# Mixing weights fetched as rows from DRAM in place of 48 transposes, with the order of some late work changed

## The reference

```
h = x + 0.5 * swiglu(rms_norm(x))                      # width 2816
z = rms_norm(h) @ w_in + b_in                          # aq ak av bq bk bv ga gb
ya = dilated attention, 12 heads in 3 groups           # windows 128/512/2048, dilations 1/4/16
yb = sliding-window attention, 8 query heads, sinks
merged = sigmoid(ga) * (ya @ w_branch_a) + sigmoid(gb) * (yb @ w_branch_b)
h = h + merged @ w_out
h = h + 0.5 * swiglu(rms_norm(h))
out = rms_norm(h)
```

## Time and profile before

| what | us |
|---|---|
| median of 3 runs | 2035.16 (2033.75 to 2035.31) |
| the profiled execution's own time | 2035.47 |
| its span | 2033.7 |
| PE busy | 2011.3 (99%), 9374 matmuls |
| DVE busy | 1361.3 (67%) |
| ACT busy | 784.6 (39%) |
| POOL busy | 83.7 (4%) |

### The profile page before, as it was taken

The page is one execution under the profiler, slowest core; times in us unless marked ns, Lnnn a source line. Parts: engine busy times, 40 slices in busy tenths (PEclk is TensorE's granted clock), DMA queues, the critical chain, the costliest instruction groups (busy, mean ns, idle before and its releaser), DMA issues.

```text
span 2033.7 us, 26354 instructions
## 1 busy us (share of the span) xinstructions
PE 2011.3 (99%) x9374; PEld 1640.7 (81%) x9374; DVE 1361.3 (67%) x2333; ACT 784.6 (39%) x1479; POOL 83.7 (4%) x94
## 2 busy tenths in 40 slices
PE   8999999999999999999999999999999999999998
PEld 6888888888888877777777888888888888888886
DVE  7986666666988455555666443458876676666986
ACT  6343333334455243334454112135433333334453
POOL 1000000000012100100100000000000000000021
PEclk9999999999999999999999999999999999999999
DMA  5233333258544311101114111114233323267433
GB/s 187 78 120 124 120 132 108 92 173 282 158 126 151 105 39 45 34 32 43 48 58 145 55 53 47 48 46 150 99 109 109 104 99 109 78 228 251 142 95 128
DMA packets 97563, 221.23 MB, mean 109 GB/s; under 512 B 20159, under 2 KB 20195, under 8 KB 95648
## 3 DMA queue, kind: packets, MB, share of 16 engines
q1 hardware_dynamic: 69568, 164.66, 24.5%
q10 hardware_dynamic: 22800, 46.29, 6.7%
q0 software_dynamic: 5072, 8.68, 1.3%
HBM read 164.41 MB, written 59.08 MB: 110 GB/s over the span
## 4 chain that ended last, share of the span: by engine, by line
PE 95%; DVE 3%; ACT 1%; issue 1%; DMA 0%; ACTq 0%; DVEq 0%; SPq 0%
PE bank L2017 20%; PE bank L2019 20%; PE bank L2018 20%; PE bank L1953 10%; PE bank L1955 10%; PE bank L1954 10%; PE bank L2184 2%; PE bank L2221 2%; PE bank L2197 1%; DVE op_l L1386 0%; DVE gs_l L1420 0%; PE bank L2234 0%; PE bank L1977 0%; DVE hg L1608 0%; DMA gate<-ffn_in 0%
## 5 line engine op out<-in xcount | busy, mean ns | idle before, releaser
L2017 PE MATMUL bank<-B_h,op_h 128*128 128x512 f32 x624 | 246.3, 395 | 9.5 <-DVE op_l L1386 7.7
L1953 PE MATMUL bank<-xh,wh 128*128 128x512 f32 x640 | 255.4, 399 | 0.0
L1955 PE MATMUL bank<-xh,wl 128*128 128x512 f32 x640 | 249.6, 390 | 0.0
L1954 PE MATMUL bank<-xl,wh 128*128 128x512 f32 x640 | 249.6, 390 | 0.0
L2017 PE MATMUL bank<-T_h,op_h 128*128 128x512 f32 x640 | 249.1, 389 | 0.0
L2018 PE MATMUL bank<-T_l,op_h 128*128 128x512 f32 x640 | 249.0, 389 | 0.0
L2019 PE MATMUL bank<-T_h,op_l 128*128 128x512 f32 x640 | 249.0, 389 | 0.0
L2018 PE MATMUL bank<-B_l,op_h 128*128 128x512 f32 x624 | 243.9, 391 | 0.0
L2019 PE MATMUL bank<-B_h,op_l 128*128 128x512 f32 x624 | 243.9, 391 | 0.0
L2017 PE MATMUL bank<-gs_h,op_h 128*128 128x512 f32 x616 | 240.6, 391 | 0.7 <-DVE gs_l L1420 0.7
L2019 PE MATMUL bank<-gs_h,op_l 128*128 128x512 f32 x616 | 239.7, 389 | 0.0
(11 more groups left out here) (211 smaller groups left out, 3381.3 us busy)
## 6 DMA issues: line engine op xcount, KB each, us to landing
gr<-g_ops SPq DMA_DIRECT2D x154, 256.0 KB, 2.7
raw<-stream SPq DMA_DIRECT2D x56, 512.0 KB, 3.5
gate<-ffn_in SPq DMA_DIRECT2D x44, 512.0 KB, 4.0
up<-ffn_in SPq DMA_DIRECT2D x44, 512.0 KB, 4.9
g_ops<-tT SPq DMA_DIRECT2D x78, 256.0 KB, 2.0
g_ops<-gb SPq DMA_DIRECT2D x58, 256.0 KB, 5.1
A<-ffn_down ACTq DMA_DIRECT2D x6, 1536.0 KB, 7.2
h_spill<-h ACTq DMA_DIRECT2D x32, 256.0 KB, 2.8
```

The costliest lines, as they stand in the source:

```text
L1953: nc.tensor.matmul(out, wh[slot][:, cols], hi, start=first, stop=False)
L1954: nc.tensor.matmul(out, wh[slot][:, cols], lo, start=False, stop=False)
L1955: return nc.tensor.matmul(out, wl[slot][:, cols], hi, start=False, stop=last)
L2017: nc.tensor.matmul(out, op_h[slot][:, cols], hi, start=first, stop=False, skip_group_check=True)
```

## The change

1. The 12 groups of four transposes and POOL's 12 copies go. Once per pair, PE transposes the [128, 48] alphas once (event `turn`), DVE copies the result out of bank 7 (`turned`), ACT writes it to DRAM (`mix rows`, at the end of slot (3, 3) or (6, 3)), and POOL fetches for each of the 12 steps a tile of [128, 512] with each row read by 64 partitions (two DMAs of 64 partitions). DVE multiplies `og` by that tile (event `x`); two tiles are used in turn. The multiplications are moved to other slots (`MIX_AT`).
2. The job of slot (8, 3) goes to slot (9, 0).
3. Branch-A products of t = 0 and 1 are made inside the last attention slots (event `a`), the last three chunks' `pv` uses banks 7 and 6 in turn, and the branch products of the first merge step use two banks each.
4. ACT's and DVE's split of the next step's first weight unit moves from t = 1 to t = 2, ahead of the loads of `h`.
5. In both FFNs the first half of B22's low part moves from j = 36 to 35, T2 and T3 of m = 1 from 35 to 36, T4 from 36 to 37.
6. Of the seven additions of squares for the first half of the norm after ffn(0), the last four go from POOL to DVE (t = 59 to 62).

```diff
-MIX_AT = {(3, 3): ((0, 0), (0, 1)), (4, 2): ((0, 2),), (4, 3): ((1, 0), (1, 1)), (5, 2): ((1, 2),),
-          (6, 3): ((2, 0),), (7, 0): ((2, 1),), (7, 1): ((2, 2),), (7, 2): ((3, 0),), (7, 3): ((3, 1),), (8, 0): ((3, 2),)}
-Y_AT = {(4, 3): 0, (5, 3): 1, (7, 2): 2, (8, 2): 3}
+MIX_AT = {(4, 0): ((0, 0),), (4, 1): ((0, 1),), (4, 2): ((0, 2),), (4, 3): ((1, 0),), (5, 0): ((1, 1),), (5, 1): ((1, 2),),
+          (7, 0): ((2, 0), (2, 1)), (7, 1): ((2, 2),), (7, 2): ((3, 0),), (7, 3): ((3, 1),), (8, 0): ((3, 2),)}
+Y_AT = {(4, 3): 0, (5, 3): 1, (7, 3): 2, (8, 2): 3}
+LATE_JOBS = ((1, 1, 1, 0), (1, 0, 1, 0), (1, 0, 0, 0))
+A_BANK, B_BANK = (0, 1, 0, 1), (2, 3, 2, 3)
...
-            n_jobs = (1, 2, 1, 2)[s] if u < A_UNITS else 1 if u < HEAD_UNITS - 1 else (0, 0, 1, 0)[s] if u < HEAD_UNITS else (1, 0, 0, 0)[s]
+            n_jobs = (1, 2, 1, 2)[s] if u < A_UNITS else 1 if u < HEAD_UNITS - 2 else LATE_JOBS[u - HEAD_UNITS + 2][s]
...
+            if s == 3 and pair is not None:
+                misc.append(("m", "turn", pair))
+            misc += [("x", n // 2, n % 2, g) for n, g in MIX_AT.get((u, s), ())]
...
+            if c == CHUNKS + 1:
+                plan.append(("a", 0))
             if 0 <= c - PV_LAG < CHUNKS:
                 plan.append(("pv", c - PV_LAG))
+            if c == CHUNKS - 1 + PV_LAG:
+                plan.append(("a", 1))
...
+            if s == 3 and pair is not None:
+                plan.append(("mix", "rows", pair))
...
+def pv_bank(c):
+    return 7 if c in (CHUNKS - 3, CHUNKS - 1) else 6
...  (POOL)
-            add_squares(1, 0)
+            add_squares(1, 0, DVE_SQUARES)
...
-                pool.wait_ge(alpha_made, pair + 1)
+                pool.wait_ge(rows_kept, 16 * (pair + 1))
...
                         if k >= 2:
-                            pool.wait_ge(m_done, M_INDEX[("m", "mix", (k - 2) // 6, (k - 2) // 3 % 2, (k - 2) % 3)] + 1)
-                        nc.gpsimd.tensor_copy((wide_0 if k % 2 == 0 else wide_1)[:],
-                                              e[:, g, 4 * hf:4 * hf + 4, :].unsqueeze(3).to_broadcast([P, 4, 2, HD])).then_inc(wide_done, 1)
+                            pool.wait_ge(mixed, k - 1)
+                        for a in range(2):
+                            pool.dma_start(wide[k % 2][a * HD:(a + 1) * HD],
+                                           bass.AP(tensor=alpha_rows.tensor, offset=alpha_rows.offset + P * (6 * QT * pair + 2 * QT * g + 8 * hf + a),
+                                                   ap=[[0, HD], [2 * P, 4], [1, P]])).then_inc(wide_in[k % 2], 16)
...  (ACT)
+                elif e[:2] == ("mix", "rows"):
+                    pair = e[2]
+                    act.wait_ge(m_out, M_INDEX[("m", "turn", pair)] + 1)
+                    act.dma_start(alpha_rows[pair], turned[pair][:]).then_inc(rows_kept, 16)
...
                         if t == 2:
+                            split_high(unit + MERGE_UNITS, 0, 0, (part_done, 8))
...  (DVE)
-                                           (36, "B22", 0), (36, "B22", 1)):
+                                           (35, "B22", 0), (36, "B22", 1)):
...
-                    for first, x, m in ((17, "T1", 0), (21, "T2", 0), (21, "T3", 0), (22, "T4", 0), (31, "T1", 1), (35, "T2", 1), (35, "T3", 1),
-                                        (36, "T4", 1)):
+                    for first, x, m in ((17, "T1", 0), (21, "T2", 0), (21, "T3", 0), (22, "T4", 0), (31, "T1", 1), (36, "T2", 1), (36, "T3", 1),
+                                        (37, "T4", 1)):
...
+                        if 59 <= t <= 62:
+                            add_squares(1, 0, (DVE_SQUARES + t - 59,))
...
+                elif e[0] == "x":
+                    pair, hf, g = e[1:]
+                    k = 6 * pair + 3 * hf + g
+                    part = og[3 * pair + g][:, hf * HALF:(hf + 1) * HALF]
+                    dve.wait_ge(pv_out, 4 * (3 * pair + 3))
+                    dve.wait_ge(wide_in[k % 2], 32 * (k // 2 + 1))
+                    nc.vector.tensor_tensor(part, part, wide[k % 2][:].rearrange("p n t -> p (n t)"), ALU.mult).then_inc(mixed, 1)
...  (PE)
+                elif e[0] == "a":
+                    t = e[1]
+                    pe.wait_ge(w_low, TILES + 1)
+                    pe.wait_ge(y_low, 4)
+                    pe.wait_ge(job_scaled, 2 * TILES - 1 + t)
+                    branch_a(A_BANK[t], 0, t).then_inc(a_done, 1)
...
-                    if c:
+                    if c >= CHUNKS - 3:
+                        pe.wait_ge(pv_out, c - 1)
+                    elif c:
                         pe.wait_ge(pv_out, c)
...
+                        pe.wait_ge(alpha_made, e[2] + 1)
+                        last = nc.tensor.transpose(bank[7][0:6 * QT, 0:P], alpha[e[2]][:].rearrange("p g n a -> p (g n a)"), ident[:])
...
-                    for part in (1, 3) if first_step else range(4):
+                    for part in ((3,) if t < 2 else (1, 3)) if first_step else range(4):
...
+                            elif t >= 2:
+                                pe.wait_ge(mul_done, 5 * (t - 2) + (2 if part == 1 else 4))
```

More of the change, by code:

```diff
@@ L444, in build @@
     least = [place(f"least{p}", [P, QT, 2], at(Y[2] + 2) + 1024 * p + 448) for p in range(2)]
+    turned = [place(f"turned{p}", [6 * QT, P], at(Y[2] + 2) + 1024 * p + 512) for p in range(2)]
     total = [place(f"total{p}", [P, QT, 2], at(Y[2] + 2) + 1024 * p + 512) for p in range(2)]
@@ L1750, in _ @@
             for e in PLAN:
[L1751 removed]
+                if e[0] in ("exp", "a") or e[0] == "t" and e[1] >= 4 * A_UNITS:
                     continue
@@ L1888, in merge_step @@
                             dve.wait_ge(sig_done, 2 * job + gate + 1)
-                            dve.wait_ge(part_done, 4 * job + 2 * gate + 2)
-                            nc.vector.tensor_tensor(z[:], z[:], bank[2 * gate + 1][:], ALU.mult).then_inc(mul_done, 2)
+                            if t < 2 and gate == 0:
+                                dve.wait_ge(a_done, t + 1)
+                            else:
+                                dve.wait_ge(part_done, 4 * job + 2 * gate + 2)
+                            nc.vector.tensor_tensor(z[:], z[:], bank[(B_BANK if gate else A_BANK)[t]][:], ALU.mult).then_inc(mul_done, 2)
                         dve.wait_ge(mul_done, 5 * job + 4)
@@ L1894, in merge_step @@
                         nc.vector.tensor_tensor(gl[:, tile, cols], tmp[2][:], gh[:, tile, cols], ALU.subtract).then_inc(m_low, 1)
-                        if hf and not tile:
+                        if t == 2:
                             split_low(unit + MERGE_UNITS, 0, 0)
@@ L1970, in project, with branch_a @@
                     last = product(out, slot, k, normed(k, hf), n == 0, n == KT - 1)
+                return last
+            def branch_a(out, slot, hf):
+                cols = slice(hf * HALF, (hf + 1) * HALF)
+                for p in range(2):
+                    last = product(bank[out][:], slot, p, (yah[p][:, cols], yal[p][:, cols]), p == 0, p == 1)
                 return last
@@ L2158, in _ @@
             for e in PLAN:
-                if e[0] in ("mix", "w", "exp", "den", "tables"):
+                if e[0] in ("mix", "x", "w", "exp", "den", "tables"):
                     continue
@@ L2220, in _ @@
                             moving = keys[:, 2 * a:2 * a + 2, :].rearrange("p i k -> p (i k)")[:, at_key:at_key + width]
-                            last = nc.tensor.matmul(bank[6][a * HD:(a + 1) * HD, to:to + width],
+                            last = nc.tensor.matmul(bank[pv_bank(c)][a * HD:(a + 1) * HD, to:to + width],
                                                     values[:, tile, a * HD:(a + 1) * HD], moving,
```

59 lines of the change are left out of this document (25 added, 34 removed).

## The result

The changed kernel took 2023.13 us (median of 4 runs, 2021.34 to 2024.77), the kernel before beside it 2035.22 (4 runs, 2033.75 to 2035.31): ratio 0.9943, interval 0.9931 to 0.9955. Forecast: 2023.4, range 2020.3 to 2028.5. The profiled execution took 2024.77, its span is 2022.9.

What follows compares the result with a forecast made beforehand. The prediction took PE to bound the kernel, with 95% of the chain of waits. Gains of 6.0 + 2.0 + 1.3 + 1.8 + 0.7 = 11.8 us took the median from 2035.16 to 2023.4, range 2020.3 to 2028.5.

Steps and rivals of the forecast that it cites:

- cover of 5 us for late gathers: Attention: DVE has some 5 us to spare before PE asks for its results, so late gather tiles stay hidden.
- time line of the chain: Pair 1's alphas: write issued after slot (6, 3)'s `exp`, landed at 995.5; first tile at 999.3; DVE waits 2.9 us.
- The 2.5: First merge: output products begin at about 1107.7 in place of 1110.25, 2.5 us earlier.
- the wait for `ybl`: Last chunk's `pv`: its 1.1 us wait goes, through the A product ahead and differing banks.
- the 1.2 given back: Merge, output product d = 4: PE must wait for DVE's first addition to `h`, losing 1.2 us.
- Low parts turning into waits: Rival, chance 0.13: parts 5 and 6 gain nothing and lose up to 2.5 us, giving 2028.4.
- Gathers late: Rival, chance 0.10: late tiles hold up the attention loop; landing in 7 us costs 4 us, giving 2027.4.
- the price for slow gathers: Attention, pair 1: about L - 6 us lost for the first tile and each of about three later, L being landing time.
- the turning point of L = 9.5: Rival, chance 0.04: from about 9.5 us gather landing time, both pairs' losses exceed 11.8 us, making the kernel slower.

Runs made afterwards that it cites:

- e5: Changed kernel with 48 unread transposes put back on PE, four at each multiplication by the weights; median 2029.78 us.
- e8: Changed kernel with pair 1's gathers held back on POOL until PE has done the projection job of slot (7, 1); median 2032.49 us.
- e7: Changed kernel with pair 1's gathers held back on POOL until PE has done the `t` of slot (7, 0); median 2023.86 us.
- e3: Changed kernel with the projection job back in slot (8, 3) and none in (9, 0) and (9, 1); median 2025.11 us.
- e4: Changed kernel with the last three chunks' `pv` all in bank 6, each waiting for the drain before; median 2022.94 us.
- e14: Changed kernel with one merge bank for all B products and one for the A products of t = 1 to 3; median 2022.97 us.
- e11: Changed kernel with the first branch-A product moved behind the last `pv`, banks unchanged; median 2022.10 us.
- e9: Changed kernel with the two loads of `h` issued later, behind the wait for t = 2's sum; median 2026.82 us.

## Why the prediction was right

The time was right within 0.3 us, and that much closeness is luck. The steps sum to 13.6 against 11.8, every part but the first came out above its forecast, and start and end of the sampled executions took part of it back. Nor did the forecast know that the kernel before has two groups of times. What was right is the mechanism: PE is the chain, each part takes off it the matmuls or the late starts that it was said to, and no new wait of PE shows.

- *Part 1*, forecast 6.0, measured 5.75, with the rule of the earlier trace rows (time to the next instruction's start, not the instruction's own duration) confirmed by e5. One reading of these rows was wrong: the `t` at 857.67 is eight transposes and not six, so the group behind it had cost 1.70 - 8 x 0.109 - 0.09 = 0.74 and not 0.95, most of the difference. Of the cover of 5 us for late gathers e8 confirms 4.8 for `den`, while e7 finds only 3.3 for the `pv` drain. The time line of the chain was wrong by some 4 us, to the good: I let ACT's DMA wait for the activations before it in the program.
- *Part 2*, forecast 2.0, measured 2.15 in the traces and 2.14 in e3, with the clock back at 0.76 once both waits are back. The times say that the clock does not fall in every execution; where it does not, the part is worth about 0.9.
- *Part 3 and 4*, forecast 2.5 less 1.2, measured 2.64 less 0.22. The 2.5 were right in size (e4 and e14: 1.3 and 1.4). One reason was wrong: the prediction credited the wait for `ybl` to the A product ahead and the banks together, and e4 and e11 give it to the banks. The step that failed is the 1.2 given back. The prediction took the load of `h` to last as before. From its issue to the first addition it took 10.9 us before and 9.66 after. What differs is the load of 512 KB of weights, issued by SP 2.9 us behind it before and 4.0 in e9, where `h` took 10.6, but 5.5 in the changed kernel. The packets in the traces bear it out: until the first half of `h` had landed, SP's queue moved 0.52 MB in the kernel before and in e9, and 0.09 MB or less in the changed kernel and in the ten experiments that load `h` as it does, where the landing took 9.2 to 9.6 us. At 386 to 396 GB/s (1099 to 1104 us, after) half a megabyte is 1.3 us. I moved one transfer and left its neighbour unexamined. No run varied the weights' load alone.
- *Part 5*, forecast 1.8, measured 2.3; *part 6*, forecast 0.7, measured 0.99. Both took the wait as the profile lists it. The true price was higher each time: 0.9 cost 1.15, 0.7 cost 0.99, 1.1 cost 1.31, 1.0 cost 1.40, 0.4 cost 0.55. The first product behind a wait also takes longer to its successor (0.31 in place of 0.23 us behind the wait of 0.7 in e9), which is a part of it.
- *The rivals.* Low parts turning into waits: none did. Gathers late: not in the changed kernel, where the slowest landed in 5.2 us. e8, with the first issue for pair 1 13.5 us late, pays once and still beats the kernel before (ratio 0.9988, 0.9979 to 0.9997). That bounds a late issue; the price for slow gathers, once per tile, and the turning point of L = 9.5 stay untested.

The Trainium skill, SBUF - State Buffer, section "SBUF: two separate sides", on the shared port: the twelve multiplications took 0.68 to 0.69 us each, none beside an addition of POOL's, since each addition waits for one of them. `den` beside an addition took 2.12 us (1018.46) against 1.23 alone (984.08); that agrees. Its warning that descriptors are held up, made for VectorE's two-port modes, has no case in any run here. POOL issued three gathers from 992.87 on in 0.62 us each, as elsewhere, while DVE ran a `den` of two SBUF inputs in its usual 1.23 us (993.51), and the one pause between two issues, 4.2 us at 988.7, fell where DVE was idle for most of the time.

## What to carry to other kernels

Where one engine is the whole chain, compare two traces by the start of the same instruction along the program: steps of 0.2 us become visible that medians with 1.5 us of scatter hide. Look at the granted clock of each stretch first, though, for the same code can differ by 1.6 us from one execution to the next. Price a wait at what the profile shows and 0.15 to 0.4 us more, and at far more when the granted clock falls behind it. When an edit moves a transfer, list what else is in the queues in its time, for what moves beside it sets when it lands.

## What was not expected of the hardware

- A DMA issued by ACT does not wait for the activations before it in the program. The write of `turned` went out at 985.11, the `exp` ahead of it began at 986.17; the loads of `h` went out at 1093.87 and 1094.52, the activation for `wh` that stands before them began at 1095.03. An activation that stands behind such issues does wait for them: in e9 it began at 1096.72, after 2.06 us of idle time.
- The write of 24 KB to DRAM landed in 1.4 us (median of two), a gather of 128 KB from POOL in 3.2 (median of 24, 2.9 to 5.2), and a gather's issue took POOL 0.62.
- POOL paused between the third and the fourth gather of pair 1: for 4.2 us in the changed kernel, 2.4 in e7 and 2.3 in e8, each time until 0.4 us behind the start of DVE's first multiplication, that is, until just after the first tile had landed. No semaphore stands there. For pair 0 four went out in a row. What it waits for stays open.
- After a PE wait of 6.6 us the granted clock was 0.50 for 8 us (e8), after one of 2.7 it was 0.57 over 4 us (e9), after two of 0.8 within 2.4 us it was 0.76 over 7 us (e3). After single waits of 1.1 (e4), 1.0 (e14), 0.5 and 0.4 us it stayed at 1.00. At 24 to 28 us and in the last norm it fell in some executions and not in others, with the same code.
